# Another order and other PSUM banks for the first mixer of a two-block network

## The reference

```
h = rmsnorm(x) ; z = h @ w_in                     # 1024 -> 3208 columns
z_a, z_b, z_c, z_d = split(z)
y_a = rwkv7(z_a)      # 4 heads of 64: a recurrence with decay and a rank-one correction, token by token
y_b = mlstm(z_b)      # 4 heads: causal convolution, gates, a normalised linear recurrence
y_c = swa(z_c)        # 4 query heads: softmax over a window of 128 tokens, with a bias and a sink
y_d = fox(z_d)        # 4 heads: causal softmax over all tokens, with a forgetting gate
x = x + rmsnorm(concat(y_a, y_b, y_c, y_d) @ w_out)
```

## Time and profile before

| | us |
|---|---|
| median of 3 runs | 1654.27 (1651.79 to 1654.36) |
| the profiled execution: its own time | 1654.27 |
| its span, first to last instruction | 1652.5 |
| PE busy | 1619.0 (98%) |
| DVE, ACT, POOL busy | 820.2, 683.6, 264.1 |
| TensorE clock granted, mean | 0.996 of full speed |

### The profile page before, as it was taken

One profiled execution on the slowest core, in us unless ns is written; L12 is line 12 of the kernel. 1 busy time (PEld: TensorE's weight loads), 2 busy tenths in 40 slices (PEclk: granted clock), 3 DMA queues, 4 the chain that ended last, 5 costly groups with the idle time before them and its releaser, 6 DMA issues.

```text
span 1652.5 us, 22571 instructions
## 1 busy us (share of the span) xinstructions
PE 1619.0 (98%) x8860; PEld 1326.6 (80%) x8860; DVE 820.2 (50%) x1383; ACT 683.6 (41%) x1248; POOL 264.1 (16%) x225
## 2 busy tenths in 40 slices
PE   9998998999999999999999999999999999999998
PEld 6776776888888888888888888877877888888887
DVE  6567456476555542274444433356464444444333
ACT  7555467454444442364333333244233433333222
POOL 1232011102222210003222210000110032222000
PEclk9999999999999999999999999999999999999999
DMA  5221110313322333223232333323122332322332
GB/s 198 80 84 47 40 39 14 128 65 110 104 92 90 102 93 102 87 77 105 100 102 91 98 94 94 100 96 102 53 90 89 102 102 90 102 100 78 104 104 75
DMA packets 45984, 149.59 MB, mean 91 GB/s; under 512 B 5260, under 2 KB 8500, under 8 KB 45880
## 3 DMA queue, kind: packets, MB, share of 16 engines
q1 hardware_dynamic: 41760, 142.10, 26.6%
q10 hardware_dynamic: 4120, 6.06, 1.1%
HBM read 146.03 MB, written 2.11 MB: 90 GB/s over the span
## 4 chain that ended last, share of the span: by engine, by line
PE 91%; DVE 5%; ACT 2%; issue 1%; DMA 1%; POOL 0%; ACTq 0%; DVEq 0%; SPq 0%; POOLq 0%
PE bank L276 90%; PE bank L474 1%; DVE x L2278 1%; ACT hi L1101 0%; DVE lo L1812 0%; DMA raw<-in_w_in 0%; DVE x L2617 0%; DVE y L2273 0%; ACT sq L1120 0%; DVE yf L2273 0%; DVE acc L1828 0%; ACT pair L1184 0%; DMA raw<-in_ffn_w_gate 0%; DMA raw<-in_w_out 0%; PE bank L534 0%
## 5 line engine op out<-in xcount | busy, mean ns | idle before, releaser
L1812 DVE TENSOR_TENSOR lo<-raw,hi 128x512 fp32r<-128x512 f32 (+1 forms) x514 | 393.7, 790 | 588.2 <-ACT hi L1101 587.8
L276 PE MATMUL bank<-xh,hi 128*128 128x512 f32 (+1 forms) x1640 | 617.2, 387 | 5.2 <-ACT xh L1514 2.0
L276 PE MATMUL bank<-xh,lo 128*128 128x512 f32 (+1 forms) x1640 | 606.8, 381 | 1.4 <-DVE lo L1812 1.3
L276 PE MATMUL bank<-xl,hi 128*128 128x512 f32 (+1 forms) x1592 | 597.9, 387 | 0.0
L1101 ACT ACTIVATE hi<-raw 128x512 fp32r<-128x512 f32 (+1 forms) x540 | 321.4, 616 | 452.6 <-PE bank L276 411.4
L276 PEld LDWEIGHTS bank<-xh,hi 128*128 128x128 f32 x1640 | 303.6, 188 | 74.5 <-issue 6.9
L276 PEld LDWEIGHTS bank<-xh,lo 128*128 128x128 f32 x1640 | 302.9, 188 | 62.0 <-DVE lo L1812 2.4
L276 PEld LDWEIGHTS bank<-xl,hi 128*128 128x128 f32 x1592 | 298.9, 188 | 62.3 <-issue 3.1
L276 PE MATMUL bank<-fH,hi 128*128 128x512 f32 (+1 forms) x572 | 213.6, 373 | 0.0
L276 PE MATMUL bank<-fH,lo 128*128 128x512 f32 (+1 forms) x572 | 213.2, 373 | 0.0
L276 PE MATMUL bank<-fL,hi 128*128 128x512 f32 (+1 forms) x572 | 213.2, 373 | 0.0
(11 more groups left out here) (405 smaller groups left out, 1103.8 us busy)
## 6 DMA issues: line engine op xcount, KB each, us to landing
raw<-in_ffn_w_up SPq DMA_DIRECT2D x88, 512.0 KB, 3.5
raw<-in_w_in SPq DMA_DIRECT2D x50, 512.0 KB, 3.5
raw<-in_ffn_w_down SPq DMA_DIRECT2D x48, 512.0 KB, 3.5
raw<-in_ffn_w_gate SPq DMA_DIRECT2D x44, 512.0 KB, 3.4
raw<-in_ffn_w_down SPq DMA_DIRECT2D x24, 384.0 KB, 3.1
raw<-in_w_out SPq DMA_DIRECT2D x16, 512.0 KB, 3.5
x<-in_xt SPq DMA_DIRECT2D x8, 256.0 KB, 6.0
x<-in_xt ACTq DMA_DIRECT2D x8, 256.0 KB, 5.1
```

Of the source, the lines that this page charges most:

```text
L276: return pe.matmul(out, w, x, start=start, stop=stop, skip_group_check=True)
L1812: dve.tensor_tensor(k.lo[i % CUT][:, 0:w], k.raw[u % RAW][:, at:at + w], k.hi[i % CUT][:, 0:w].bitcast(F), SUB).then_inc(k.cut_tail[i % 2], 1)
```

## The change

The change replaces the two tables `ORDER1` and `BANKS1` by others. No function, no constant beside them and no instruction's operands other than the bank numbers are changed. The order within each chain stays the same, and so does the number of steps of each. Two lines of the first table and two of the second stand for the rest:

```
--- before
+++ after
 ORDER1 = """
-a r0 a r0 r1 a r0 a r0 k1 a p r1 m r1 c1 p r0 a c1 r0 m r1 a m r0 r1 k0 r1 m r0 r0 r1 r0 k0 m r1 r0 c1 r1 r0 r1 m
+r1 a r0 r1 k1 a r0 r1 a r0 r1 a r0 r1 p a r0 r1 k1 p a r0 r1 a r0 m r1 r0 k0 r1 m r0 r1 m r0 r1 m r0 k0 m r1 r0 m
...
 BANKS1 = {
-    "m": "307432543244317557524767",
+    "m": "742465765324627545436552",
```

More of the change, by code:

```diff
@@ L59 @@
 ORDER1 = """
-p p p p a p p p p p p p p r0 p a p p a p r0 p p r0 p p r0 p a p p r0 p p r0 p p r0 a p k0 p k0 a p p r0 p a a r1 p
-p p c0 p r0 r1 c0 p a p r0 r1 c0 c1 p p c0 p r0 c1 a c0 p r0 p r1 a r1 p r1 r0 a a r1 a p r1 r0 a p r0 a r1 k1 r0
-a r0 a r0 r1 a r0 a r0 k1 a p r1 m r1 c1 p r0 a c1 r0 m r1 a m r0 r1 k0 r1 m r0 r0 r1 r0 k0 m r1 r0 c1 r1 r0 r1 m
-f00 r0 m r1 p p m r1 r0 r1 m r0 m f01 f00 m r1 f01 k1 p p p r1 a m a r1 m f01 a p a r1 k1 m a m r1 r1 a p f00 m
-f10 r1 a p r1 m a m f10 p a m r1 a f11 p s f10 s m s a f11 f11 s m s s s s s a o o s o o o o o o o
+p p a p p p p p p p p p p a p r0 p p r0 p a p r0 p a p p p p a r0 p p a p r0 p p p a p p r0 r0 k0 p k0 p r1 p a p
+c0 r0 p r1 a p c1 c0 r0 p c0 r0 r1 a c1 p c0 r0 p p c0 c1 p r0 r1 p c1 a p a a r0 r1 p a c1 r0 p r1 a r1 r0 p a r0
+r1 a r0 r1 k1 a r0 r1 a r0 r1 a r0 r1 p a r0 r1 k1 p a r0 r1 a r0 m r1 r0 k0 r1 m r0 r1 m r0 r1 m r0 k0 m r1 r0 m
+r0 r1 f00 r0 m r0 r1 m f00 f01 r1 p m k1 p r1 f00 f01 p m r1 p r1 f01 p a a m a r1 m k1 a m r1 f10 p a m r1 a m a
+m r1 f10 p p a m r1 p f10 p s s s a m r1 m a f11 m a f11 m a f11 s s s s s s o o s o o o o o o o
 """.split()
 BANKS1 = {
-    "a": "3234751522462523754675265726742546427460263432763247425635713273261653122606342",
-    "m": "307432543244317557524767",
[L71 to L78, removed]
+    "a": "4446564575376537376542377562243735422573257264372543237563756257624167207426014",
+    "m": "742465765324627545436552",
+    "r0": "5673245674534532656327736346542642644375676764264335745",
+    "r1": "2677226425423752336524263543535737264267326734743664431",
+    "k0": "32672675",
+    "k1": "65355257",
+    "f00": "234",
+    "f01": "476",
+    "f10": "535",
+    "f11": "373",
 }
```

## The result

| | before | after |
|---|---|---|
| median, us (6 runs each) | 1653.22 (1651.79 to 1654.36) | 1663.49 (1660.06 to 1668.37) |
| ratio to before, 95% interval | | 1.0054 (1.0037 to 1.0072) |
| the profiled execution, us | 1654.27 | 1660.60 |
| its span, and its mean granted clock | 1652.5, 0.996 | 1658.8, 0.995 |

The new order is slower, by about 0.5%. The forecast was 1649.0, its range ended at 1655.0.

A forecast was written before the change was run, and what follows sets the result against it. PE, busy 98% of the span, bounds the kernel. Gains 1.6 + 3.1 + 0.4 + 0.8 + 0.2 + 1.6 = 7.7 us, less 2.4 for new waits, leave 5.3: from 1654.27 to 1649.0 us, range 1644.8 to 1655.0.

The forecast's parts named there:

- the prediction's signs: Idle time from 128 to 172 us under 2.5 us; longest wait before L645; o.1 starting 5 us earlier than 293.5.
- sign of being wrong: More than five bank waits in the softmax rounds, or a second stretch at the lower clock, would make the prediction wrong.
- 45 to 128 us: First mixer, projection steps placed otherwise; PE has no idle time there, so costed at nothing.
- 128 to 148 us: First mixer, more steps between r1.4, r1.5 and r1.6; idle time from 1.97 to 0.4 us, gain 1.6.
- 148 to 172 us: Softmax rounds, mostly two steps between rounds; idle time from 4.07 to 1.0 us, gain 3.1.
- 184 to 204 us: Behind m.2's transfers on ACT's queue; 0.9 us of waits instead of 1.31, gain 0.4.
- 204 to 255 us: Stretch of the first mixer that the prediction left out, since PE had no idle time there.
- 255 to 275 us: The full softmax, 0.59 us idle; similar cover on both sides, gain 0.2.
- The end: 275 to 306 us: products L2072 run without POOL's xl, o.1 starts 11.3 us after m.18; gain 1.6.
- The reserve: Four unseen new waits of 0.6 us, set against the gains: 2.4 us.
- The clock: 184 to 204 us: with fewer waits ahead the clock may stay up; half of 1.7 us taken, gain 0.8.
- The slower rival: 128 to 175 us: r0 and r1 in step, both queued on DVE, nine rounds lose waits; +9, 1663, chance 0.13.

The follow-up runs named there:

- h3_late: Kernel before with the new order and banks from its 141st to its 204th step alone; median 1663.6 us, ratio 1.0053.
- h1_front: Kernel before with the new order and banks in its first 55 steps alone; median 1653.9 us, ratio 1.0009.
- e6_before_s_ahead: Kernel before with p.57, s.0, s.1 and s.2 moved ahead of a.31 and m.18, banks as before; median 1656.4 us, ratio 1.0019.
- h7_tail: Kernel before with p.57 and s.0 to s.2 ahead of a.31, and the new order and banks from the 205th step on; median 1661.7 us, ratio 1.0044.
- the middle: Kernel before with the new order and banks from its 56th to its 140th step alone; median 1655.5 us, ratio 1.0013.
- x1_p_late: Kernel before with projection steps p.48 and p.49 moved 9 steps later, behind f01.0; median 1659.8 us, ratio 1.0033.
- e7_p45_cover: Changed kernel with projection step p.45 put back behind a.14, where it stood before; median 1664.7 us, ratio 1.0063.
- e3_filler: Changed kernel with unread identity transposes on PE, 8 ahead of r1.6 and 18 ahead of k1.3; median 1663.2 us, ratio 1.0063.
- x2_late_p_early: h3_late with projection steps p.48 and p.49 put forward, behind r1.19, as they stood before; median 1670.4 us, ratio 1.0097.

## Why the prediction was wrong, step by step

Two steps failed above all. The sum had no term for the stretch from 204 to 283 us apart from a gain of 0.2, since PE had had no wait in most of it: it loses 3.0 us at equal clock (h3_late). And the clock had one term, a gain of 0.8: the mean over the runs is a loss of 4.4. Of the prediction's signs, PE's idle time from 128 to 172 us fell to 4.6 us and not under 2.5; the longest wait is the 2.65 us before `k1.3`, not L645's; and `o.1` starts 5 us later than 293.5, not 5 earlier. Its own sign of being wrong, a second stretch at the lower clock, came.

The rows of the end in the changed kernel: the source view of line 2072, then PE's timeline with the waits before `a.33`, `m.20` and `o.1`:

```profile
L2072 DVE TENSOR_TENSOR bias<-bias,small x4: 417/418/424, 292.4 to 293.4; 128x256 f32<-128x256 f32 x4
...
289.96 0.32 PE L276 MATMUL bank<-acc,values 128*64 128x128 f32 x1 [0.98 <-DVE acc L1960]
...
293.89 1.09 PE L645 MATMUL bank<-cA,bias 128*128 128x128 f32 x8 [1.38 <-DVE bias L2072]
...
298.60 0.47 PE L276 MATMUL bank<-xh,hi 128*128 128x512 f32 x1 [1.96 <-issue]
```

Step by step:

- **45 to 128 us, costed at nothing.** Failed: 1.3 us. The step was "PE has no idle time there, no chain step moves nearer"; there is a new wait of 0.8 us, for DVE's L1892, and projection steps that were in runs stand alone. h1_front confirms 1.3.
- **128 to 148 us, 0.4 us left.** Failed: 1.82 us are left, and about 0.35 more are hidden in `r1.5`, whose second product starts when DVE has left its bank (140.93, 140.99), 0.65 us behind the first; in the kernel before the two start 0.29 us apart. The order was read on PE alone; `c1.4`, which has no PE work, had moved on ACT to a place right ahead of an eviction that PE needs.
- **148 to 172 us, 1.0 us left.** Right direction, mis-sized: 2.78 us are left. One wait of 1.40 us is `r1.7`'s, which starts at 157.16; its bank 4 held a product of `r0.15` that DVE copied out until 157.06, behind its work of a softmax round.
- **184 to 204 us.** Right, and better than said: 0.28 us of idle time and full clock. The transfers' wait was covered, and two of them took 0.94 us instead of the 1.89 of the earlier trace rows.
- **204 to 255 us, not in the sum.** This is the main failure: from the 140th to the 204th step the profiled executions lose 5.1 us, 2.65 of them the wait before `k1.3` and 1.7 the clock behind it. I had looked only at stretches in which PE had waited before. h3_late alone has a median 10 us above before's beside it.
- **255 to 275 us.** Right: no idle time.
- **The end, a gain of 1.6.** The mechanism of its first half was right: L2072 takes 0.42 us each (417/418/424 ns, against the earlier trace rows), with no `xl` work beside it. The rule of the Trainium skill ("SBUF — State Buffer", section "Who interferes with whom"), by which DVE's products run free once POOL reads nothing beside them, gave the same, and the trace agrees. `m.20` starts 7.2 us behind `m.18`'s end (said: 7.4), behind waits of 0.98 and 1.38 us (said: 2.6 in all). But the step "that DVE work covers itself" failed: `o.1` waits 1.96 us, behind two table loads on ACT, and starts 11.9 us behind `m.18`, not 11.3. From the 204th step to `o.8` the profiled executions lose 0.5 us instead of gaining; e6_before_s_ahead and h7_tail show that the remainders ahead of the power slow other work of DVE and that PE waits elsewhere.
- **The reserve**, four new waits of 0.6 us, was too small: 0.85, 1.33, 1.96 and 2.65 us came.
- **The clock** had one term, +0.8. That fall did go. The new falls cost 4.4 us in the mean, net of it, and no term stood for them.

The slower rival named 1663, which is the median, but by a mechanism that is not there: from 128 to 172 us PE waits 4.6 us, less than before, not 12.

Shown: the waits before `k1.3`, `r1.6` and `o.1` with their causes, the share of the front, middle and late parts of the order, and that the middle and the late part, each put in alone, lower the mean clock. Only suggested, by one edit over five runs with a small new wait beside it: that taking projection steps out of a stretch of light work lowers it. Open: what exactly lowers it, and how much of the last 1.3 us (4.1 less the 2.8 of the three parts) the end holds.

## What to carry to other kernels

Where one engine is busy all the time, the stretches in which it does not wait are what a new order can lose, and they need the same reading as the waits. A moved step takes its work on every engine with it, above all a table load on the activation engine: follow the steps that have no work on the bottleneck too. Compare two orders at equal clock and at the clock that they get, over many runs.

## What the runs showed of the hardware

- **One program, several clocks.** The kernel before takes 1651.7 to 1660.6 us, following its mean granted clock. Falls of the clock in the first mixer last 3.4, 6.8, 10.2, 13.7 or 17.1 us in the traces.
- **A busy PE does not hold the clock.** It fell at 208 us in x1_p_late and e7_p45_cover, where PE was busy for 3.54 and 4.00 of the 4 us from 204, and at 219 us in h1_front with 4.00 of 4, and stayed low for 13.7 to 17.1 us with PE busy throughout. (Busy is by the profile; it does not say how full the array is.) The work ahead has few rows or few columns (32 rows x 512, 128 x 65, 128 x 64), but the same work stood in the kernel before and in the changed one without a fall at that place in their profiled executions. The Trainium skill ("TensorE: Matmul & The Clock Gate", section "What's actually happening") ties the clock to how busy PE has been; PE's busy time in these traces does not tell when it falls.
- **Transposes as filler**, eight of 128 x 128 in a wait of 1.33 us, did not hold it at 146 us (e3_filler).
- **POOL's work slows some of DVE's and not other.** Beside POOL's `xl` a product L2072 took up to 1485 ns instead of 411, a cast of 128 x 512 1.49 us instead of 0.43; a maximum over 128 x 512 out of PSUM took as long as without it (1.26 us for two in e6_before_s_ahead, 1.29 in the kernel before, where POOL was idle for most of it).
- **A table load on ACT takes 1.28 us**, every one in these rows; in x2_late_p_early three of them stood within 6 us, behind them DVE, and behind DVE PE for 6.17 us.
